# The gather reads the residual in fp32, and one and a half pieces of expert 16 are loaded ahead of the expert loop

## What is computed

```python
x = x + mix @ w_out[l]
h = rms_norm(x, norm_ffn_w[l])
x = x + hierarchical_moe(h, ...)
return rms_norm(x, norm_final_w)

# in hierarchical_moe, xt = h as (256, 2048):
for e in range(N_EXPERTS):                      # 32
    he = jax.nn.silu(xt @ w1[e]) * (xt @ w3[e]) # (2048 x 512) each
    y = y + combine[:, e:e + 1] * (he @ w2[e])  # (512 x 2048)
```

## Time and profile before

| what | value |
|---|---|
| median of three runs | 1478.21 us (1477.36 to 1479.08) |
| the profiled execution | 1476.32 us |
| its span, first to last instruction | 1474.5 us |
| PE, PEld busy | 1355.0 us (92%), 834.6 us (57%) |
| DVE, ACT, POOL busy | 612.2 us (42%), 440.0 us (30%), 65.1 us (4%) |
| read from HBM | 478.96 MB |
| granted TensorE clock, mean | 0.979 of full speed |

### The profile page before, as it was taken

One profiled execution on the slowest core, in us unless ns is written; L12 is line 12 of the kernel. 1 busy time (PEld: TensorE's weight loads), 2 busy tenths in 40 slices (PEclk: granted clock), 3 DMA queues, 4 the chain that ended last, 5 costly groups with the idle time before them and its releaser, 6 DMA issues.

```text
span 1474.5 us, 20318 instructions
## 1 busy us (share of the span) xinstructions
PE 1355.0 (92%) x7740; PEld 834.6 (57%) x7740; DVE 612.2 (42%) x1136; ACT 440.0 (30%) x865; POOL 65.1 (4%) x63
## 2 busy tenths in 40 slices
PE   5999999999999798899999999899899889899885
PEld 3899999999988653343353353353353344335332
DVE  5977787778864611232223212212222122222223
ACT  5465655656654411111021011111111111111102
POOL 0012221022100000000000000000000000000000
PEclk9999999999999999999999999999999999999998
DMA  7565555555546759999999999999999999999994
GB/s 204 151 156 151 147 148 151 128 149 144 200 143 212 309 230 430 426 428 428 427 428 429 428 428 428 429 425 425 428 429 428 428 429 428 427 428 429 428 428 173
DMA packets 147064, 481.63 MB, mean 327 GB/s; under 512 B 11385, under 2 KB 112978, under 8 KB 121810
## 3 DMA queue, kind: packets, MB, share of 16 engines
q1 hardware_dynamic: 147026, 481.10, 83.5%
HBM read 478.96 MB, written 2.12 MB: 326 GB/s over the span
## 4 chain that ended last, share of the span: by engine, by line
PE 67%; DMA 24%; DVE 5%; ACT 2%; issue 1%; SPq 1%; DVEq 0%; ACTq 0%
PE bank L562 65%; DMA ew<-in_expert_w_dram 23%; PE bank L565 2%; DVE w_parts L1430 1%; ACT ew L1342 1%; DMA mixT<-in_x_dram 1%; SPq L529 0%; ACT fw_r L1269 0%; DVE ew L1469 0%; DVE fw L1889 0%; ACT fw L1009 0%; DVE fw_r L1750 0%; DVE fw L1390 0%; DVE fw L1940 0%; DVE ew L1897 0%
## 5 line engine op out<-in xcount | busy, mean ns | idle before, releaser
L562 PE MATMUL bank<-ew,hT 128*64 128x512 f32 (+1 forms) x1568 | 466.7, 602 | 39.5 <-DMA ew<-in_expert_w_dram 32.0
L562 PEld LDWEIGHTS bank<-ew,hT 128*64 128x64 f32 (+1 forms) x1568 | 157.1, 141 | 336.1 <-issue 335.9
L562 PE MATMUL bank<-act_parts,w_parts 128*128 128x256 f32 x2304 | 308.1, 288 | 1.7 <-DVE w_parts L1430 1.7
L562 PEld LDWEIGHTS bank<-act_parts,w_parts 128*128 128x128 f32 x2304 | 285.2, 191 | 2.9 <-issue 1.4
L562 PE MATMUL bank<-ew 128*64 128x512 f32 (+2 forms) x1120 | 248.8, 574 | 6.8 <-DVE ew L1899 6.8
L562 PE MATMUL bank<-mixT,hT 128*64 128x512 f32 x512 | 227.0, 596 | 0.0
L1897 DVE SCALAR_TENSOR_TENSOR ew<-ew,bank 128x256 f32<-128x256 f32 x32 | 13.5, 421 | 453.9 <-ACT ew L1344 453.9
L562 PEld LDWEIGHTS bank<-ew 128*64 128x64 f32 (+1 forms) x1120 | 84.8, 141 | 147.5 <-issue 137.2
L1430 DVE TENSOR_TENSOR w_parts<-fw,w_parts 128x2048 fp32r<-128x2048 f32 x64 | 147.8, 2313 | 31.5 <-ACT w_parts L1031 30.5
L1359 ACT ACTIVATE ye_r<-bank 64x512 fp32r<-64x512 f32 x128 | 68.8, 585 | 279.7 <-PE bank L562 278.9
L1342 ACT ACTIVATE ew<-bank,gs 128x512 f32<-128x512 f32 x32 | 22.0, 687 | 422.1 <-PE bank L562 422.1
(11 more groups left out here) (243 smaller groups left out, 1084.3 us busy)
## 6 DMA issues: line engine op xcount, KB each, us to landing
ew<-in_expert_w_dram SPq DMA_DIRECT2D x160, 2048.0 KB, 16.2
mixT<-in_expert_w_dram SPq DMA_DIRECT2D x32, 2048.0 KB, 18.6
fw<-in_w_in_dram SPq DMA_DIRECT2D x48, 1024.0 KB, 5.9
fw<-in_w_out_dram SPq DMA_DIRECT2D x16, 1024.0 KB, 5.0
mixT<-in_x_dram SPq DMA_DIRECT2D x1, 2048.0 KB, 7.4
fw<-in_x_dram SPq DMA_DIRECT2D x1, 2048.0 KB, 9.7
out_dram<-fw SPq DMA_DIRECT2D x4, 512.0 KB, 2.7
hT<-decay_rows SPq DMA_DIRECT2D x8, 192.0 KB, 5.8
```

What stands on the lines that cost most here:

```text
L562: return nc.tensor.matmul(o, l, r, start=start, stop=stop, skip_group_check=True)
```

## The change

The gather takes the residual `x2` itself as stationary operand, in fp32, through a view `xk` whose 128 columns of one k lie 16 elements apart. It needs 4 matmuls a group instead of 8, each of two records. `high_rows`, `low_rows` and their two semaphores are gone. As later rounds of the loop would gather again, the experts' sums now go to a copy of the residual, `acc`, which ACT writes (`keep`, four copies, contiguous), and the last norm and the output read `acc`. `gather_first` makes groups 0 to 3 and `gather_second` 4 to 7, and the first expert of a quad waits for `xT` two k at a time.

The freed SBUF takes piece 0 and the first half of piece 1 of expert 16 (`ahead`), loaded once, behind expert 0's pieces 0 and 1. In the loop SP issues for expert 16 only the second half of piece 1 and pieces 2 to 5, and PE reads the rest from `ahead`. The router weights move to `cst` and are issued a little earlier.

```diff
-        hn_hi = [fw_r[:, D:2 * D], fw_r[:, 2 * D:3 * D]]
-        hn_lo = [misc_r[:, 0:D], fw_r[:, 0:D]]
+        acc = fw[:, 0:2 * D].rearrange("p (t d) -> p t d", t=NT)
+        xk = x2.rearrange("q t (p k) -> q t k p", k=KD)
+        ahead = [fw[:, 2 * D:4 * D], misc[:, 0:D]]
...
                 if m == 10:
-                    sp.wait_ge(s_proj, NH * 6 + 7)
+                    sp.wait_ge(s_atm, NH * (LEVELS - 1))
+                    sp.wait_ge(s_aq, NH)
...
             load_expert(0, 1)
+            sp.wait_ge(s_y, NH)
+            sp.dma_start(ahead[1], expert_piece(AHEAD, 1)[:, 0:D]).then_inc(s_ahead, 16)
+            sp.wait_ge(s_proj, NH * 6 + 8)
+            sp.wait_ge(s_restD, NH * 6 + 15)
+            sp.dma_start(ahead[0], expert_piece(AHEAD, 0)).then_inc(s_ahead, 16)
...
+                sp.wait_ge(s_ed, (r * NE + AHEAD - 1) * 6 + 1)
+                sp.nop().then_inc(s_ew[0], 16)
+                sp.wait_ge(s_ed, (r * NE + AHEAD - 1) * 6 + 2)
+                sp.dma_start(ewp[1][:, D:], expert_piece(AHEAD, 1)[:, D:]).then_inc(s_ew[1], 16)
+                for piece in range(2, 6):
+                    sp.wait_ge(s_ed, (r * NE + AHEAD - 1) * 6 + piece + 1)
+                    load_expert(AHEAD, piece)
...
                 for c in range(2):
-                    for lo in range(2):
-                        for t in range(NT):
-                            k = 2 * g + c
-                            l = mm(o[:, c * T:(c + 1) * T], (hn_lo if lo else hn_hi)[t][:, k * P:(k + 1) * P],
-                                   pickr[:, t, :, 0:P], lo == 0 and t == 0, lo == 1 and t == NT - 1)
+                    for t in range(NT):
+                        l = mm(o[:, c * T:(c + 1) * T], xk[:, t, 2 * g + c, :], pick[:, t, :, 0:P], t == 0, t == NT - 1)
...
-                for g in range(5):
+                for g in range(4):
                     gather_group(bank[FIRST[g]], g)
...
-                for g in range(5, 8):
+                for g in range(4, 8):
...
-                        if j == 0:
-                            pe.wait_ge(s_xeA, n * 4 + 2 + 2 * half)
-                            pe.wait_ge(s_xeD, n * 4 + 2 + 2 * half)
...
                         for k in range(KD // 2):
+                            if j == 0 and k % 2 == 0:
+                                pe.wait_ge(s_xeA if k % 4 else s_xeD, n * 4 + 2 * half + k // 4 + 1)
...
-            act.wait_ge(s_restD, NH * 6 + 15)
-            high_rows(1, 0, 96)
+            act.wait_ge(s_restD, NH * 6 + 16)
+            for t in range(NT):
+                keep(t, 0, 3 * 512)
...
-            dve.wait_ge(s_hnH, 4)
-            low_rows(1, 96, P)
...
-                    V.tensor_tensor(x2c, x2c, bank[COMB[i % 4]][:, :], ALU.add).then_inc(s_add[t], 1)
+                    V.tensor_tensor(ac, ac, bank[COMB[i % 4]][:, :], ALU.add).then_inc(s_add[t], 1)
```

More of the change, by code:

```diff
@@ L58 @@
 NQUAD = NE // QUAD
+AHEAD = NE // 2
 C_ID = 0
@@ L540, in _ @@
             with sp.Fori(0, rounds) as r:
-                with sp.Fori(1, NE) as e:
+                with sp.Fori(1, AHEAD) as e:
+                    for piece in range(6):
+                        sp.wait_ge(s_ed, (r * NE + e - 1) * 6 + piece + 1)
+                        load_expert(e, piece)
+                sp.wait_ge(s_ed, (r * NE + AHEAD - 1) * 6 + 1)
[5 more added lines that the diff above has]
+                    load_expert(AHEAD, piece)
+                with sp.Fori(AHEAD + 1, NE) as e:
                     for piece in range(6):
@@ L940, in places, with up_weights, quad @@
                 l.then_inc(s_placeT_mm, 1)
-            def quad(n, q, first, last):
+            def up_weights(piece, k, ahead_of):
+                if ahead_of and piece == 0:
+                    w = ahead[0]
+                elif ahead_of and piece == 1 and k < KD // 4:
+                    w = ahead[1]
+                else:
+                    w = ewp[piece]
+                return w.rearrange("p (k n) -> p k n", n=FF)[:, k, :]
+            def quad(n, q, first, last, has_ahead=False):
                 for j in range(QUAD):
@@ L957, in quad @@
                                        xT[:, half * 8 + k, j * SLOTS:(j + 1) * SLOTS],
-                                       ewp[half * 2 + which].rearrange("p (k n) -> p k n", n=FF)[:, k, :],
+                                       up_weights(half * 2 + which, k, has_ahead and j == 0),
                                        half == 0 and k == 0, half == 1 and k == KD // 2 - 1)
@@ L995, in _ @@
                 quad(pe.snap(r * NQUAD), 0, True, False)
-                with pe.Fori(1, NQUAD - 1) as q:
+                with pe.Fori(1, AHEAD // QUAD) as q:
+                    quad(pe.snap(r * NQUAD + q), q, False, False)
+                quad(pe.snap(r * NQUAD + AHEAD // QUAD), AHEAD // QUAD, False, False, True)
+                with pe.Fori(AHEAD // QUAD + 1, NQUAD - 1) as q:
                     quad(pe.snap(r * NQUAD + q), q, False, False)
@@ L1266, in _, with keep @@
                 high_out(m)
-            def high_rows(t, lo, hi):
-                act.activation(hn_hi[t].rearrange("q (k p) -> q k p", k=KD)[:, :, lo:hi],
-                               x2[:, t].rearrange("q (p k) -> q k p", k=KD)[:, :, lo:hi], ACT.Copy).then_inc(s_hnH, 1)
+            def keep(t, lo, hi):
+                act.activation(acc[:, t, lo:hi], x2[:, t, lo:hi], ACT.Copy)
+            act.wait_ge(s_tri, 1)
             def row_squares(n, t):
@@ L1303, in _ @@
                                ACT.Copy).then_inc(s_h2T, 1)
-            high_rows(1, 96, P)
+            for t in range(NT):
+                keep(t, 3 * 512, D)
             act.wait_ge(s_gex, 1)
@@ L1761, in _ @@
                     rest_out(m)
-            for t in range(NT):
-                dve.wait_ge(s_hnH, t + 1)
-                low_rows(t, 0, 96)
             def add_last(t):
```

51 lines of the change are left out of this document (19 added, 32 removed).

## The result

The changed kernel takes **1513.22 us** (median of 4 runs, 1509.87 to 1519.38), the kernel before beside it 1477.78 (1476.66 to 1479.08): ratio 1.0248, 95% interval 1.0225 to 1.0272. It is slower, as forecast, but by 35.4 us instead of 22; the median lies 0.2 us above the range. The profiled execution took 1512.96, its span is 1511.2, 36.7 more than before.

A forecast was written before the change was run, and what follows sets the result against it. The prediction took the DMA weight queue as the bound, idling when PE releases late around gathers. Loop 16.4 + start 5.5 + preload 0 = +21.9 us on 1476.3, adjusted by 1.9 to 1500; range 1495 to 1506, 8 in 10 1490 to 1513.

The forecast's parts named there:

- What bounds: Loop: the DMA queue bounds; late PE releases around each gather leave it idle once its 3.8 us reserve is passed.
- The lead of 2.5 us: Loop stretches: a fresh weight request needs 2.5 us until it moves data, from 7.4 us issue to landing less 4.9.
- The gather: Gather as fp32: 64 records of 0.215 us, 13.76 us instead of 8.6, +5.15 each; seven loop stretches cost 16.4 us.
- rival 1: Gathers: the strided weight load sets their pace, 1.5 us more each, 1512 us in all; chance 0.15.
- the lower end: Gather's strided weight load: stays beneath 0.215 us a record and costs nothing.
- my 7.6: Each of seven loop stretches: the gather's 5.15 us plus the 2.5 us until a fresh issue moves data.
- The start: Before half 1 of expert 0: longer gathers, less one low_rows, delay it 5.5 us with no reserve; +5.5 us.
- The preload: Expert 16's pieces loaded ahead: 7.35 us of transfer is free, but becomes queue idle time before the late release; 0.
- rival 2: Loop stretches: the clock stays up because waits for weights get shorter; 1493 us in all, chance 0.22.
- rival 3: Loop: PE bounds instead of the queue, so every gather counts whole; 41.5 us more, 1520 us, chance 0.04.
- rival 4: Loop: the gather fits the reserve (below 12.4 us) and the preload pays; 1471 or 1476 us, chance 0.05.
- rival 5: Start alone costs, loop gathers hidden and preload lost; 1484 us, chance 0.04.

The follow-up runs named there:

- b_late: Kernel before, only SP changed: pieces 0 and 1 of the second expert of quads 1 to 6 requested later, no PE work added; 1503.36 us.
- b_loop: Kernel before with only the loop's seven gathers done in fp32 on the strided rows; 1504.28 us, ratio 1.0185.
- half_no_ahead: Changed kernel without the load ahead, the loop's gathers over the first token tile only (32 records instead of 64); 1483.62 us.
- g48: Changed kernel without the load ahead, 48 of the 64 records in each loop gather; 1499.26 us, ratio 1.0145.
- contig: Changed kernel with the gather's stationary operand as 128 columns side by side instead of 16 elements apart; 1505.74 us, ratio 1.0207.
- b_start: Kernel before with only the gathers ahead of and inside expert 0 done in fp32 on the strided rows; 1482.35 us, ratio 1.0031.
- no_ahead: Changed kernel without the loads ahead, expert 16 loaded in the loop like every other expert; 1513.21 us, ratio 1.024.
- ahead18: Changed kernel with the 1.5 pieces loaded ahead for expert 18 instead of expert 16; 1507.64 us, ratio 1.0206.
- half_ahead18: Changed kernel with the loop's gathers over the first token tile only and the load ahead for expert 18; 1477.66 us, ratio 1.0006.
- half_ahead16: Changed kernel with the loop's gathers over the first token tile only, load ahead kept for expert 16; 1483.27 us, ratio 1.004.

## Why the prediction was right in kind and wrong in size

**What bounds.** Right, and shown: the late request costs (b_late), the kernel's other edits do not (b_loop), and the cost disappears with a shorter stretch (half_no_ahead).

**The lead of 2.5 us: the step that failed most.** I took it from the shortest issue to landing, 7.4 us, and wrote length + 5.15 + 2.5 - 39.2. The line above says 3.7 in place of 2.5, 7 x 1.2 = 8.4 us; the changed kernel's own seven steps, 29.2 us over seven times 117.5, make it **8.1 us**. The 2.5 is right for a request that comes when the queue is empty. Three issues of the changed kernel, each by itself, in microseconds to landing: piece 4 of expert 8 at 773.03, issued 0.6 us after the last landing; then the pieces 0 of experts 9 and 13, issued 1.7 and 1.9 us ahead of the landing before them:

```profile
DMA to landing us min/median/max: 7.3/7.3/7.3
...
DMA to landing us min/median/max: 7.6/7.6/7.6
...
DMA to landing us min/median/max: 8.8/8.8/8.8
```

A gather is followed by two such interruptions, ahead of piece 4 and again ahead of the next expert's piece 0, and the second left holes of 0.7 to 2.0 us where a lead of 2.5 would have left 0.4 to 0.8. b_late has only one, and its six quads lost 25.9 us on 243.5 us of stretches: a lead of 2.9 us. Nor is all of the 8.1 us lateness: 2.8 of it are holes in the later part of three quads, at pieces asked for 6 us or more ahead. The kernel before has such holes too, two in the loop's quads, and what makes them is open. About the gather itself the lead is 3.3 us. Why a request that comes while the previous piece still moves takes longer is open as well; it does not always, as g48 has one 2.1 us ahead with a hole of 0.2.

**The gather.** I had 13.76 us, it is 14.46 from its first record to the next row's start: 0.46 by the strided load (contig), 0.24 by its ends, since I left the last record's tail out. An undisturbed stretch grew by 5.85 instead of 5.15, 4.9 us in seven; as low clock added 6.8 us to these stretches instead of 7.3, the sum came to **+4.3** over mine. So my range's upper end and my rival 1 had the right mechanism, 0.46 us where I gave it 1.5, and my argument for the lower end, that PE's own row stays under 215 ns, was wrong: that row's 201 ns was for 4 elements between columns, at 16 elements the mean is 305. I also set the 201 ns of transposes against 142 ns of other transposes. The old gather's own weight loads, of fp32r with columns side by side, already took 203 in the loop:

```profile
L562 PEld LDWEIGHTS bank<-act_parts,fw_r 128*128 128x128 f32 x336 | 52.9, 203 | 4.2 <-DVE hT L1878 3.8 <-ACT hT L1332 0.4
```

My 60 ns on top of that row are 263, above 215, and would have pointed to rival 1. The Trainium skill, "Advanced Engine Details and Errata", section on memory cachelines, has a penalty for an access that goes to another 16-byte line each time; 305 ns against 190 agree. That 4 and 16 elements apart are alike was my reading of it; the two strides stand here in different instructions, 201 and 305 ns, and no run tried both in one.

Together 16.4 + 4.3 + 8.1 = 28.8, less 1.7 by which the seven quads of the kernel before exceed 117.5 us themselves, 27.1; measured 27.4. The difference is my 7.6, which is 7.65 rounded and makes 0.35 in seven. The sum closes because the 8.1 was taken from these quads; the test of the corner is the other kernels, whose 34 long stretches give 35.5 without the changed kernel's six.

**The start.** I had +5.5, it is +7.8 (the other profiled kernels with this start: 539.64 to 541.41, so +5.4 to +7.2). Two windows of the changed kernel, columns as before:

```profile
518.00:521.40 3.40, 3.40 (x10) 2.64 (x9) 0.88 (x2) 0.00 (x0) 0.00 (x0) 0.50 0.00 0
521.50:525.80 4.30, 4.30 (x21) 4.17 (x19) 0.87 (x2) 0.84 (x2) 0.00 (x0) 1.00 0.00 0
```

1.2 GHz held until 521.4 instead of 519, and the first gather took 9.8 us, not 8.7; the second 7.3 instead of 6.9; and the gather began 0.4 later instead of 0.35 earlier. That is 2.3 us. The last of these is no answer on `low_rows`: in the eight other profiled kernels with this start the gather begins at 514.41 to 515.97, in the five with the old one at 515.69 to 516.93. By b_start 6.6 of the 7.8 are the gather and the clock. How much is the clock, two other executions show: g48, with the changed kernel's start, and b_late, with the start of the kernel before. A window of each:

```profile
518.90:522.00 3.10, 3.10 (x16) 3.10 (x15) 0.52 (x2) 0.84 (x2) 0.00 (x0) 1.00 0.00 0
...
518.00:521.30 3.30, 3.30 (x17) 3.30 (x17) 0.88 (x2) 0.55 (x2) 0.00 (x0) 0.50 0.03 5
```

Where the full clock came back at 518.9, the changed start costs 540.05 - 534.20 = 5.9 us, close to my 5.5. Where 1.2 GHz held until 521.4, the old start alone came 1.6 us later, at 535.79. So some 2 us of the +7.8 are one execution's clock. The copies and the router's move were not tried alone; the 1.2 us over b_start bound them, together with the clock.

**The preload** at nothing: right (no_ahead), and it pays where I said the queue bounds (ahead18, half_ahead18). With a short gather I let 3.8 of the 7.35 us through at full clock; half_ahead16's step shows 1.7: the holes about its gather sum to 4.4 us, where I had 3.5, and two later ones in the quad to 1.4.

**The clock.** I expected the same four low stretches; the tail's +1.6 is one that fell into expert 31's half 1. My rival 2 (the waits shorten, the clock stays up) is refuted: the changed kernel waited 33.9 us and had four low stretches as before, and in the execution with six of seven (g48) PE waited 34.3 us, less than before.

**The bounds.** PE alone (rival 3) is refuted by b_late, a gather inside the reserve (rival 4) by the stretches, the start as the only cost (rival 5) by b_loop. The range needed a lead measured under the conditions in question, with 7 us on its upper end.

## What to carry to other kernels

Where a queue with one buffer a piece runs beside an engine, add up the stretch from one landing to the request that the queue will need last, and compare it with the pieces between: below the corner work is free, above it every us counted here, and the mean room elsewhere does not help. Try a load ahead where the queue is the longer side, not behind the latest release; the same 3 MB were worth nothing at one expert and 6 us two experts on. A kernel that has used up such a reserve also turns every dip of the clock in its stretch into time. That this widens the spread of its runs is likely but not shown: the changed kernel's four runs spread over 9.5 us and the four of the kernel before beside it over 2.4, but eight of the kernel before over 6.1 and four of b_loop over 2.4.

## What the runs showed of the hardware

- A weight load of 128 fp32 columns 16 elements apart takes 305 ns, side by side 190; beside fp32 records of 256 columns this shows as 0.221 against 0.216 us a record.
- A 2 MB piece lands 7.1 to 7.8 us after its issue when the queue is empty (37 issues of all kernels here). Issued 1.6 to 2.2 us ahead of the previous landing it took 7.6 to 8.8 us in the changed kernel and 7.1 to 9.7 in all (43 issues). Issued 4 us ahead or more it followed without a hole in 328 of 341 cases of the kernel before and the changed one; the holes of the other 13 were 0.15 to 1.6 us, their cause is open.
- The clock fell to 1.2 GHz in half 1 of a last expert, behind PE's wait of 2.3 to 2.7 us for piece 3, in four of seven quads of the changed kernel, in six of seven of g48 and in two of seven of contig. In the changed kernel's other three quads it stayed up behind the same half 0 and a wait of 2.4 us. A short dip made a stretch 1.7 us longer, the longest one 4.9 (g48).
